# Modulation of shift and scale on VectorE with output channels on partitions, and the start of the first mixer in eighths

## The chip, the core and the metric

One core of a Trainium2 chip runs the whole program. The metric is the device time of one execution in microseconds (us), from a profile of the hardware; three executions are timed, and their median counts.

## The reference

Two decoder layers on 256 tokens of 2048 channels, all float32. A condition vector c modulates each half layer:

```python
cond = silu(c)                                        # 2048
mod = cond @ w_mod[l] + b_mod[l]                      # 2048 x 12288, one product per layer
sh1, sc1, g1, sh2, sc2, g2 = split(mod, 6)
u = x * (1 + sc1) + sh1
proj = u @ w_in[l]                                    # 2048 x 6144: q, k, v, conv gates
# rotary, 8 heads of dilated attention; 8 groups of a gated 3-tap convolution; group RMS norm
x = layer_norm(alpha * x + (1 + g1) * (mixed @ w_out[l]))
u = x * (1 + sc2) + sh2
x = layer_norm(alpha * x + (1 + g2) * (relu(u @ w_ff1[l]) ** 2 @ w_ff2[l]))
```

The matrix w_mod alone is 201 MB, a third of all that is read. Its product is with one vector: each weight is used once.

## The kernel before

**Units, groups and positions.** Every large product is cut into units of 512 output columns. A unit has 8 groups; a group takes one slice of the weights (128 x 1024, 512 KB: two blocks of 128 rows) for both token tiles. TensorE multiplies in three terms, high x high, low x high and high x low, so a group is 12 products of 512 columns (`group`, L1312, products at L1323 to L1325). ScalarE rounds a slice to w_hi (L480), VectorE subtracts to get w_lo (L793); both work four groups ahead (`ahead`). Groups of a layer's mixer are numbered p = 8 * unit + group, and everything beside the groups (rotary, heads, mod steps, slab sums) is put at such a position by hand-written lists: `QK_END`, `Q_AT`, `K_AT`, `HEAD_AT`, `O_AT` (L94 to L102), `MOD_AT` from `mod_positions` (L71), `RED_AT` from `red_positions` (L123). Each engine goes through the positions in this order.

**Modulation.** w_mod is cut into 24 slabs of 1024 output columns, 12 a layer, in 16 chunks of 128 input rows (128 x 1024, 512 KB). Input rows are on partitions. `mod_step` (L799) is one VectorE instruction a chunk: chunk times the column of cond, added to mod_acc (L808; the first of a slab is L804). A slab's 16 steps depend on each other. Then a sum over partitions is still to be made by TensorE. For shift and scale slabs that is `reduce_slab` (L1397): 8 products of 128 x 128 by a column of ones, L1403, two instructions each in the trace; VectorE adds the bias (`reduced`, L832). For the 8 gate slabs (4, 5, 10, 11, 16, 17, 22, 23) it is `gate_slab` (L1407), two products that leave the sum on all partitions, read by `gate_sum` (L839). mod_acc has two halves by turns. The later 20 slabs run through four buffers (mod_raw) that POOL's queue fills, one chunk behind each step that frees one.

**The start.** The first product needs the whole of sh1 and sc1 of layer 0, 4 slabs, so the first mixer begins with `start_units` (L1469): units 0 to 2 run side by side in three pairs of banks, and u comes in quarters. Slab q of the start holds shift and scale of 512 channels; with it 4 blocks of u can be made, and 6 groups (2 of each unit) can run. 64 chunks pass through eight buffers. VectorE does 58 of them as steps; TensorE does 6 directly from the chunk (`start_chunk`, L1431, L1439). `start_fill` (L1462) transposes x, makes the slab's sum (`start_sum`, L1443, L1448) and transposes the second half; `start_scale` (L1010) on VectorE, `start_job` (L506) on ScalarE and `start_low` (L857, L851) turn it into u_hi and u_lo. TensorE waits for u_lo of its block. Within a quarter VectorE's next steps are laid around that by `START_STEPS` and `start_quarter` (L1021).

**Queues.** SyncE's queue carries x, small tables and all layer weights; its first weight slice waits for the fourth mod step (`sp.wait_ge(mod_used, 4)`, L386), later slices for w_lo to free one of four raw buffers. POOL's queue carries w_mod. ScalarE's carries norm gains and gate biases. ScalarE's first work is four weight slices, and only then the first shift and scale of u.

## Time and profile before

| | us |
|---|---|
| median of 3 runs (2360.51, 2363.70, 2363.77) | 2363.7 |
| the profiled execution | 2359.7 |
| its span, first to last instruction | 2358.0 |
| TensorE busy | 2275.1 |
| VectorE busy | 1727.1 |
| ScalarE busy | 1101.9 |
| first product of a group starts at | 42.59 |
| mean granted TensorE clock, share of full | 0.990 |
| moved by DMA | 623 MB, mean 264 GB/s |

The span is what the profiler sees of the instructions; 1.7 us of the execution lie around it. The busy time of an engine is a sum over stages with different limits, so it is read by stage. In timelines a row's second number is how long the instruction (or the run of equal ones, xN) lasted; the start of the next one may come before it has ended, since the engines overlap neighbours. "Idle before" is the time the engine did nothing ahead of it, and the arrow names what ended it.

### The profile page before, as it was taken

Reading aid. Unit: us, or ns where it says so; the run is one execution under the profiler, and the core shown is the slowest. Engines: PE = TensorE matmul, PEld = TensorE weight load, DVE = VectorE, ACT = ScalarE, POOL = GpSimd, SP = SyncE. Lnnn points to the kernel's source line nnn. Section 1 sums busy time; section 2 is a strip of 40 time slices with the busy share of each in tenths; the row PEclk is TensorE's granted clock in tenths of the full one; section 3 lists DMA queues with packets and bytes.
Section 4 is the critical chain, followed back from the end, with each engine's and each line's share of the span. In section 5 each row is a group of like instructions: output and inputs, shape, how many; then the busy total and the mean of one; then the engine's idle time right before and its main releaser. Section 6 shows DMA issues by size and latency. Waiting matters only on the chain.

```text
span 2358.0 us, 30332 instructions
## 1 busy us (share of the span) xinstructions
PE 2275.1 (96%) x10480; PEld 1884.4 (80%) x10480; DVE 1727.1 (73%) x1929; ACT 1101.9 (47%) x1392; POOL 227.3 (10%) x400
## 2 busy tenths in 40 slices
PE   3899999999999999999999999999999999999997
PEld 2777887878888888888878888877888888888886
DVE  6889888877777777668878878777666555555566
ACT  1345543366445445435454554435553543543542
POOL 3311111110001001001010001101000000000000
PEclk9899999999999999999999999999999999999999
DMA  9987888967888888888966888886677776666574
GB/s 379 409 318 274 311 320 313 341 216 255 286 297 287 285 285 300 288 276 289 323 228 196 271 265 288 285 273 224 194 238 239 226 231 212 215 205 195 170 232 133
DMA packets 174734, 623.15 MB, mean 264 GB/s; under 512 B 19728, under 2 KB 20496, under 8 KB 174096
## 3 DMA queue, kind: packets, MB, share of 16 engines
q1 hardware_dynamic: 114128, 407.50, 50.6%
q0 software_dynamic: 55296, 201.35, 25.6%
q10 hardware_dynamic: 5184, 12.59, 1.7%
q8 instruction: 83, 1.36, 0.2%
q14 instruction: 43, 0.35, 0.0%
HBM read 619.27 MB, written 2.10 MB: 264 GB/s over the span
## 4 chain that ended last, share of the span: by engine, by line
PE 87%; DVE 6%; DMA 3%; issue 2%; ACT 1%; ACTq 0%; POOL 0%; DVEq 0%; SPq 0%; POOLq 0%
PE bank L1323 27%; PE bank L1325 26%; PE bank L1324 26%; DMA Z<-w_mod_dram 2%; DVE mod_acc L808 2%; PE bank L1428 2%; DVE w_lo L793 1%; PE bank L1337 1%; PE bank L1403 1%; PE bank L1339 1%; PE bank L1338 1%; ACT w_hi L480 1%; PE bank L1412 1%; DMA raw<-w_out_dram 0%; PE bank L1572 0%
## 5 line engine op out<-in xcount | busy, mean ns | idle before, releaser
L480 ACT ACTIVATE w_hi<-raw 128x1024 fp32r<-128x1024 f32 x764 | 807.6, 1059 | 1135.7 <-PE bank L1325 1015.2
L793 DVE TENSOR_TENSOR w_lo<-raw,w_hi 128x1024 fp32r<-128x1024 f32 x764 | 932.9, 1224 | 550.7 <-ACT w_hi L480 548.9
L1323 PE MATMUL bank<-w_hi,u_hi 128*128 128x512 f32 x1744 | 698.0, 400 | 0.3 <-DVE u_lo L851 0.3
L1325 PE MATMUL bank<-w_lo,u_hi 128*128 128x512 f32 x1744 | 684.1, 392 | 0.0
L1324 PE MATMUL bank<-w_hi,u_lo 128*128 128x512 f32 x1744 | 684.0, 392 | 0.0
L1323 PE MATMUL bank<-w_hi,m_hi 128*128 128x512 f32 x1200 | 470.9, 392 | 4.5 <-DVE m_lo L851 2.6
L1324 PE MATMUL bank<-w_hi,m_lo 128*128 128x512 f32 x1200 | 468.4, 390 | 0.0
L1325 PE MATMUL bank<-w_lo,m_hi 128*128 128x512 f32 x1200 | 468.3, 390 | 0.0
L1325 PEld LDWEIGHTS bank<-w_lo,u_hi 128*128 128x128 f32 x1744 | 330.5, 189 | 70.7
L1323 PEld LDWEIGHTS bank<-w_hi,u_hi 128*128 128x128 f32 x1744 | 330.9, 190 | 68.8 <-issue 1.4
L1324 PEld LDWEIGHTS bank<-w_hi,u_lo 128*128 128x128 f32 x1744 | 331.0, 190 | 68.0 <-issue 1.4
L808 DVE SCALAR_TENSOR_TENSOR mod_acc<-mod_raw,cond,mod_acc 128x1024 f32<-128x1024 f32 x300 | 383.6, 1279 | 0.0
L460 POOL DMA_DIRECT2D mod_raw<-w_mod_dram x316 | 167.0, 528 | 1735.7 <-DVE mod_acc L808 1455.9
L1323 PEld LDWEIGHTS bank<-w_hi,m_hi 128*128 128x128 f32 x1200 | 226.0, 188 | 53.3 <-DVE m_lo L851 3.4
L1325 PEld LDWEIGHTS bank<-w_lo,m_hi 128*128 128x128 f32 x1200 | 226.1, 188 | 47.3
L1324 PEld LDWEIGHTS bank<-w_hi,m_lo 128*128 128x128 f32 x1200 | 226.1, 188 | 46.6 <-issue 0.2
L808 DVE SCALAR_TENSOR_TENSOR mod_acc<-Z,cond,mod_acc 128x1024 f32<-128x1024 f32 x54 | 69.2, 1282 | 13.4 <-DMA Z<-w_mod_dram 11.3
L851 DVE TENSOR_TENSOR m_lo<-utmp,m_hi 128x512 fp32r<-128x512 f32 x72 | 49.1, 691 | 12.8 <-ACT m_hi L504 12.8
L1428 PE MATMUL bank<-idn,Z 128*128 128x128 f32 x416 | 54.1, 273 | 1.2 <-DVE Z L1170 1.1
L1428 PEld LDWEIGHTS bank<-idn,Z 128*128 128x128 f32 x416 | 48.4, 140 | 8.5 <-DVE Z L1170 1.7
L504 ACT ACTIVATE m_hi<-utmp 128x512 fp32r<-128x512 f32 x72 | 45.6, 633 | 2.3
L490 ACT ACTIVATE utmp<-bank 128x512 f32<-128x512 f32 x64 | 37.2, 581 | 0.0
(144 smaller groups left out, 1138.3 us busy)
## 6 DMA issues: line engine op xcount, KB each, us to landing
raw<-w_ff_dram SPq DMA_DIRECT2D x512, 512.0 KB, 4.2
mod_raw<-w_mod_dram POOLq DMA_DIRECT2D x320, 512.0 KB, 5.6
raw<-w_in_dram SPq DMA_DIRECT2D x192, 512.0 KB, 5.3
Z<-w_mod_dram POOLq DMA_DIRECT2D x64, 512.0 KB, 11.0
raw<-w_out_dram SPq DMA_DIRECT2D x64, 512.0 KB, 6.1
gate<-b_rows_dram ACTq DMA_DIRECT2D x4, 1024.0 KB, 5.0
Z<-ln_g_dram ACTq DMA_DIRECT2D x16, 256.0 KB, 6.5
Z<-ln_b_dram ACTq DMA_DIRECT2D x16, 256.0 KB, 7.3
```

The lines of the kernel that those rows point to most:

```text
L460: pool.dma_start(mod_raw[:, k:k + 1, :], chunk(r * MODS + (first + k))).then_inc(mod_in[k], 16)
L480: nc.scalar.activation(weights(w_hi, u_hi, unit, j), raw[:, j % RAW, :], ACT.Copy).then_inc(hi_ready, 1)
L490: nc.scalar.activation(utmp[:, slot, :], tb[bank][:], ACT.Copy).then_inc(t_read[bank], 1)
L504: nc.scalar.activation(dst[:, chunk:chunk + 2, :], utmp[:, slot, :], ACT.Copy).then_inc(split_hi, 1)
L793: nc.vector.tensor_tensor(weights(w_lo, u_lo, unit, j), raw[:, j % RAW, :], weights(w_hi, u_hi, unit, j).bitcast(F32), ALU.subtract).then_ ...
L808: ins = nc.vector.scalar_tensor_tensor(out=a, in0=src, scalar=cond[:, k:k + 1], in1=a, op0=ALU.mult, op1=ALU.add)
L851: nc.vector.tensor_tensor(lo[:, chunk:chunk + 2, :], src, hi[:, chunk:chunk + 2, :].bitcast(F32), ALU.subtract).then_inc(split_ready, 1)
L1323: nc.tensor.matmul(o, hi[:, k, tok], wh, start=(k == 0), stop=False)
L1324: nc.tensor.matmul(o, lo[:, k, tok], wh, start=False, stop=False)
L1325: ins = nc.tensor.matmul(o, hi[:, k, tok], wl, start=False, stop=(k == KC - 1))
L1337: nc.tensor.matmul(o[:], hi[:, k, tok], wh, start=(k == 0), stop=False)
L1428: ins = nc.tensor.transpose(b[:, c * SEQ + t * P:c * SEQ + (t + 1) * P], src(c, t), idn[:])
```

## The change

Shift and scale slabs are turned round on the host: output channels on partitions, input channels along a row. A chunk is now 128 output channels by 1024 of the 2048 inputs, so two chunks make 128 sums. A VectorE step (`column_step`) multiplies the chunk in place by half of cond laid out as a row on all partitions and adds along the row into one column of mod_part; the steps of a slab no longer depend on each other, and two small adds give the biased columns. TensorE has no part in it: `reduce_slab`, `start_chunk` and `start_sum` are gone. To have cond as a row on all partitions, TensorE makes 16 products of a broadcast column of cond by the identity (`spread_condition`) and ScalarE copies them from four banks, once, at the very beginning; the first steps wait for it.

The start goes in eighths: 8 chunks (2 blocks of shift and 2 of scale), then 3 groups, one of each unit. All 64 chunks are VectorE's. Gate slabs are computed as before, with one mod_acc in place of two; the slabs come in another order (`SLAB_ORDER`), so that two gate slabs never follow on each other too closely. The first four later chunks are at position 20 (before 17); the first mixer's mod positions now take 23, 31 and 39 too. Rotary, transposes and heads of the first group of heads move by one to two positions. POOL's start loop is a loop on the engine.

The core of the diff:

```diff
-START_LABELS = GK * START_UNITS
+START_LABELS = START_UNITS
+START_COLS = 2 * GK
+START_LAST = START_LABELS * (EIGHTHS - 1) - 1
...
-    mixer0 = ([17] * 4 + [p for p in range(18, 8 * U_MIX) if p % 8 != 7])[:MIX_SLABS[0] * KC]
+    mixer0 = ([START_LAST] * 4 + [p for p in range(START_LAST + 1, 8 * U_MIX)
+                                  if p % 8 != 7 or p < 40])[:MIX_SLABS[0] * KC]
...
-QK_END = [[(19, 21), (31, 39)], [(7, 15), (31, 39)]]
-Q_AT = [[22, 34], [14, 34]]
-K_AT = [[25, 42], [18, 42]]
-HEAD_AT = [[[27 + 2 * h for h in range(4)], [44 + 2 * h for h in range(4)]],
+QK_END = [[(21, 22), (31, 39)], [(7, 15), (31, 39)]]
+Q_AT = [[24, 36], [14, 34]]
+K_AT = [[27, 42], [18, 42]]
+HEAD_AT = [[[29 + 2 * h for h in range(4)], [44 + 2 * h for h in range(4)]],
...
-O_AT = [[43, 59], [35, 59]]
+O_AT = [[45, 59], [35, 59]]
...
-RED_NOT_BEFORE = {9: MIXER_AT[0] + 8 * U_MIX - 1, 16: MIXER_AT[1] + 8, 17: MIXER_AT[1] + 12}
+RED_NOT_BEFORE = {16: MIXER_AT[1] + 8, 17: MIXER_AT[1] + 12}
+SLAB_ORDER = [4, 6, 5, 7, 8, 9, 10, 12, 11, 13, 14, 15, 18, 16, 17, 19, 20, 21, 22, 23]
...
 def start_order(p):
-    q, i = divmod(p, START_LABELS)
-    return i // GK, GK * q + i % GK
+    e, unit = divmod(p, START_LABELS)
+    return unit, e
...
+            with pool.Fori(1, 2 * START_SLABS) as r:
+                for k in range(8):
+                    pool.wait_ge(mod_used, 8 * r + (k - 7))
+                    pool.dma_start(start_raw[:, k:k + 1, :], chunk(r * 8 + k)).then_inc(start_in[k], 16)
...
+            for i in range(4):
+                act.wait_ge(row_done, i + 1)
+                nc.scalar.activation(cond_row[:, i * NCOL:(i + 1) * NCOL], banks[i][:], ACT.Copy).then_inc(row_ready, 1)
...
+            def column_step(i, src, arrived, landed):
+                dve.wait_ge(arrived, landed)
+                half = slice(i % 2 * SLAB, (i % 2 + 1) * SLAB)
+                nc.vector.scalar_tensor_tensor(out=src, in0=src, scalar=1.0, in1=cond_row[:, half], op0=ALU.mult,
+                                               op1=ALU.mult, accum_out=mod_part[:, i:i + 1]).then_inc(mod_used, 1)
+            def column_sum(col, count, steps):
+                dve.wait_ge(mod_used, steps)
+                part = mod_part[:, 0:2 * count].rearrange("p (c h) -> p c h", h=2)
+                sync(nc.vector.tensor_tensor(mod_col[:, col:col + count], part[:, :, 0], part[:, :, 1], ALU.add))
             def mod_next(q):
+                first = START_SLABS * KC
+                src, arrived, landed = mod_raw[:, q % MODS, :], mod_in[q % MODS], 16 * (q // MODS + 1)
+                n, k = SLAB_ORDER[q // KC], q % KC
+                if n in GATE_SLABS:
+                    gate_step(k, src, arrived, (first + q, landed))
+                else:
+                    column_step(k, src, arrived, landed)
+                    if k == KC - 1:
+                        column_sum(n * SC, SC, first + q + 1)
+                        cols = slice(n * SC, (n + 1) * SC)
+                        nc.vector.tensor_tensor(mod_col[:, cols], mod_col[:, cols], mod_b[:, cols],
+                                                ALU.add).then_inc(columns_done, 1)
...
+            def start_scale(e):
+                col = START_COLS * e
+                column_sum(col, START_COLS, 2 * START_COLS * (e + 1))
...
+                nc.vector.tensor_tensor(u_shift[:, sl], mod_col[:, sh], mod_b[:, sh], ALU.add)
+                nc.vector.scalar_tensor_tensor(out=u_scale[:, sl], in0=mod_col[:, sc], scalar=1.0, in1=mod_b[:, sc],
+                                               op0=ALU.add, op1=ALU.add).then_inc(start_ready, 1)
+            def start_eighth(e):
+                def some(k0):
+                    if e + 1 < EIGHTHS:
+                        start_steps(e + 1, k0, 2)
                     else:
+                        mod_next(k0)
+                        mod_next(k0 + 1)
+                start_scale(e)
+                some(0)
+                start_low(e)
+                some(2)
...
                         for j in range(GROUPS):
                             q, i = divmod(8 * u + j, START_LABELS)
+                            if layer == 0 and q + 1 < EIGHTHS:
+                                if i < 2:
+                                    start_steps(q + 1, 4 + 2 * i, 2)
                                 if i == START_LABELS - 1:
+                                    start_eighth(q + 1)
                             ahead(base + u, j)
                             side(u, j)
...
-            start_mods(0, 0, KC)
-            dve.wait_ge(first_in, 16 * 2)
+            for i in range(2):
+                dve.wait_ge(row_ready, 2 * (i + 1))
+                start_steps(0, i, 1)
+            start_steps(0, 2, 2 * START_COLS - 2)
+            dve.wait_ge(bias_in, 16)
             prepare(0, 0)
+            start_eighth(0)
             prepare(0, 1)
-            start_quarter(0)
             prepare(0, 2)
             prepare(0, 3)
...
-            def reduce_slab(par, job, steps):
-            def start_chunk(q):
-            def start_sum(n):
...
+            def start_fill(e):
+                pe.wait_ge(x_in[e // 2], 16)
+                turn(JOB[("start turn", e)], lambda c, t: xt[:, t, (2 * e + c) * P:(2 * e + c + 1) * P])
+            def spread_condition():
+                pe.wait_ge(cond_ready, 1)
+                for i in range(4):
+                    for c in range(4):
+                        k = 4 * i + c
+                        ins = nc.tensor.matmul(banks[i][:, c * P:(c + 1) * P], cond[:, k:k + 1].to_broadcast([P, P]),
+                                               idn[:], start=True, stop=True)
+                    ins.then_inc(row_done, 1)
...
-    wm = w_mod.reshape(DEPTH, KC, P, 12 * D // 2 // SLAB, SLAB).transpose(0, 3, 1, 2, 4)
+    wm = w_mod.reshape(DEPTH, KC, P, 12 * D // 2 // SLAB, SLAB).transpose(0, 3, 1, 2, 4).reshape(SLABS, KC, P, SLAB)
+    wt = w_mod.reshape(DEPTH, 2, SLAB, 12 * D // 2 // P, P).transpose(0, 3, 1, 4, 2).reshape(SLABS, KC, P, SLAB)
+    wm = np.stack([wm[n] if n in GATE_SLABS else wt[n] for n in list(range(START_SLABS)) + SLAB_ORDER])
```

## Rows read from the trace of the kernel before

**Rows 1.** The page, busy time: engine, us, share of the span, instructions
```profile
PE 2275.1 (96%) x10480; PEld 1884.4 (80%) x10480; DVE 1727.1 (73%) x1929; ACT 1101.9 (47%) x1392; POOL 227.3 (10%) x400
```

**Rows 2.** Stretches: length, busy us and count per engine, granted clock, DMA share, GB/s
```profile
0.00:160.00 160.00, 113.30 (x524) 95.03 (x525) 127.61 (x140) 48.53 (x62) 40.34 (x80) 0.90 0.96 368
160.00:240.00 80.00, 76.15 (x368) 62.40 (x367) 73.32 (x107) 43.23 (x86) 11.60 (x22) 1.00 0.84 301
240.00:2358.00 2118.00, 2085.62 (x9592) 1726.94 (x9590) 1526.21 (x1684) 1010.12 (x1247) 175.32 (x298) 1.00 0.77 255
...
40.00:125.00 85.00, 76.06 (x351) 63.55 (x352) 73.73 (x72) 26.85 (x34) 22.63 (x43) 0.86 1.03 408
140.00:200.00 60.00, 57.25 (x274) 46.68 (x273) 56.31 (x84) 28.70 (x54) 7.92 (x15) 1.00 0.83 297
```

**Rows 3.** TensorE by line: count, busy us and mean ns, idle us before
```profile
L1403 PE MATMUL bank<-ones,mod_acc 128*128 128x1 f32 x192 | 22.1, 245 | 0.7 <-DVE mod_acc L808 0.7
...
L1439 PE MATMUL bank<-cond,Z 128*128 128x1 f32 x96 | 11.6, 250 | 2.0 <-DMA Z<-w_mod_dram 2.0
...
L1583 PE MATMUL bank<-idn,rst 128*128 128x128 f32 x64 | 7.8, 275 | 0.0
```

**Rows 4.** Timeline of TensorE at a column reduction: start us, us, what
```profile
305.52 1.84 PE L1403 MATMUL bank<-ones,mod_acc 128*128 128x1 f32 x16
307.22 0.49 PE L1323 MATMUL bank<-w_hi,u_hi 128*128 128x512 f32 x1
```

**Rows 5.** Timeline of VectorE, start units: cond, fourth step, first and last u_lo
```profile
3.42 0.17 DVE L1286 TENSOR_TENSOR cond<-cc_in,cc_e 128x16 f32<-128x16 f32 x1
...
11.49 1.28 DVE L808 SCALAR_TENSOR_TENSOR mod_acc<-Z,cond,mod_acc 128x1024 f32<-128x1024 f32 x1 [0.25 <-DMA Z<-w_mod_dram]
...
41.85 0.69 DVE L851 TENSOR_TENSOR u_lo<-utmp,u_hi 128x512 fp32r<-128x512 f32 x1 [0.56 <-ACT u_hi L517]
...
132.81 0.69 DVE L851 TENSOR_TENSOR u_lo<-utmp,u_hi 128x512 fp32r<-128x512 f32 x1 [0.34 <-ACT u_hi L517]
```

**Rows 6.** Timeline of ScalarE ahead of the first group
```profile
29.97 1.06 ACT L480 ACTIVATE w_hi<-raw 128x1024 fp32r<-128x1024 f32 x1 [1.50 <-DMA raw<-w_in_dram]
...
40.13 1.02 ACT L513 ACTIVATE utmp<-bank,u_shift,u_scale 128x256 f32<-128x256 f32 x2 [8.91 <-DVE u_scale L1018]
41.18 0.63 ACT L517 ACTIVATE u_hi<-utmp 128x512 fp32r<-128x512 f32 x1
```

**Rows 7.** Timeline of TensorE in the last start groups
```profile
130.72 0.78 PE L1323 MATMUL bank<-w_hi,u_hi 128*128 128x512 f32 x1
...
134.70 0.53 PE L1323 MATMUL bank<-w_hi,u_hi 128*128 128x512 f32 x1
...
151.64 0.39 PE L1324 MATMUL bank<-w_hi,u_lo 128*128 128x512 f32 x1
151.87 0.39 PE L1325 MATMUL bank<-w_lo,u_hi 128*128 128x512 f32 x1
```

**Rows 8.** Timeline of VectorE: small instructions, three dependent steps, steps among w_lo
```profile
39.85 0.17 DVE L1017 COPY u_shift<-mod_col 128x4 f32<-128x4 f32 x1
39.93 0.16 DVE L1018 TENSOR_SCALAR u_scale<-mod_col 128x4 f32<-128x4 f32 x1
...
61.94 4.06 DVE L808 SCALAR_TENSOR_TENSOR mod_acc<-Z,cond,mod_acc 128x1024 f32<-128x1024 f32 x3
...
224.25 1.22 DVE L793 TENSOR_TENSOR w_lo<-raw,w_hi 128x1024 fp32r<-128x1024 f32 x1
225.39 1.28 DVE L808 SCALAR_TENSOR_TENSOR mod_acc<-mod_raw,cond,mod_acc 128x1024 f32<-128x1024 f32 x1
226.59 1.22 DVE L793 TENSOR_TENSOR w_lo<-raw,w_hi 128x1024 fp32r<-128x1024 f32 x1
```

**Rows 9.** Timeline of ScalarE: an accumulator read and the next instruction
```profile
173.69 0.19 ACT L643 ACTIVATION_READ_ACCUMULATOR Z<-Z,nmx 128x1 f32 x1
173.79 0.49 ACT L643 ACTIVATE Z<-Z,nmx 128x256 f32<-128x256 f32 x1
```

More of the change, by code:

```diff
@@ L63 @@
 START_SLABS = 2 * D // SLAB
+START_X = D // NCOL
+EIGHTHS = KC // GK
 MIX_SLABS = (6, 4)
@@ L131, in red_positions @@
         out[p] = n
+    for n, later in zip(GATE_ORDER, GATE_ORDER[1:]):
+        p = next(p for p in out if out[p] == n)
+        assert p < MOD_AT[KC * SLAB_ORDER.index(later)], (n, later)
     return out
@@ L178, in transpose_jobs @@
         modded = layer < DEPTH - 1
-        if layer:
+        if layer == 0:
+            for e in range(EIGHTHS):
+                add(("start turn", e), 1)
+        else:
             add(("fill", 2 * layer), 8)
@@ L188, in transpose_jobs @@
         first, last = MIXER_AT[layer], FF_AT[layer]
-        side += [(p - first, -1, 0, "red", 2 if n in GATE_SLABS else 1, n) for p, n in RED_AT.items()
+        side += [(p - first, -1, 0, "red", 2, n) for p, n in RED_AT.items()
                  if first <= p < last]
@@ L194, in transpose_jobs @@
         side = [(8 * (8 * block + s + 1) + HID_J, "hid", 2, (block, s)) for block in range(BLOCKS) for s in range(4)]
-        side += [(p - last, "red", 2 if n in GATE_SLABS else 1, n) for p, n in RED_AT.items()
+        side += [(p - last, "red", 2, n) for p, n in RED_AT.items()
                  if last <= p < last + 8 * FF_UNITS]
@@ L897, in modulation @@
             def modulation(fill):
-                job = JOB[("red", 12 * (fill // 2) + 6 * (fill % 2) + 3)]
-                dve.wait_ge(t_read[job % 2], job // 2 + 1)
+                first = 12 * (fill // 2) + 6 * (fill % 2)
+                dve.wait_ge(columns_done, 1 + max(COLUMN_ORDER.index(first + i) for i in range(4)))
                 shift = (6 * (fill // 2) + 3 * (fill % 2)) * KC
@@ L1142, in rotate @@
                     dve.wait_ge(pair_used, 8 * base + p + 1)
+                    if layer == 0 and u == 1:
+                        dve.wait_ge(rope_ready, 1)
                     if layer == 0 and u == 0:
@@ L1395, in unit_groups, with gate_slab @@
                         side(j)
-            def reduce_slab(par, job, steps):
-                b = begin_job(job)
-                pe.wait_ge(mod_used, steps)
-                for c in range(SC):
-                    ins = nc.tensor.matmul(b[:, c:c + 1], mod_acc[:, par, c * P:(c + 1) * P], ones[:, 0:1],
-                                           start=True, stop=True)
-                ins.then_inc(t_done, 1)
-            def gate_slab(par, job0, steps):
+            def gate_slab(job0, steps):
                 for i in range(2):
@@ L1429, in turn @@
                 ins.then_inc(t_done, 1)
-            def start_chunk(q):
-                n = q // KC
-                first = q - 1 not in START_PE and all(k // KC < n for k in START_PE if k < q)
-                if first:
-                    pe.wait_ge(sum_read, n)
-                pe.wait_ge(start_in[q % 8], 16 * (q // 8 + 1))
-                for c in range(SC):
-                    ins = nc.tensor.matmul(tb[1][:, c:c + 1], start_raw[:, q % 8, c * P:(c + 1) * P],
-                                           cond[:, q % KC:q % KC + 1], start=(first and c == 0), stop=False)
-                ins.then_inc(chunk_used, 1)
@@ L1469, in start_units @@
             def start_units(side):
+                spread_condition()
                 start_fill(0)
-                for p in range(START_SLABS * START_LABELS):
+                pe.wait_ge(row_ready, 4)
+                for p in range(EIGHTHS * START_LABELS):
                     unit, j = start_order(p)
```

161 lines of the change are left out of this document (42 added, 119 removed).

## The prediction

> **What bounds the kernel now.** I read the page first, then the stretches, then the lines of each engine. The page has TensorE busy 2275.1 us of 2358.0 [rows 1], so 83 us are open. The stretches say where [rows 2]: from 0 to 160 us TensorE is busy 113.3 of 160 (46.7 open), from 160 to 240 it is busy 76.15 of 80, and in the 2118 us behind that 2085.6. Behind 240 us whatever leaves TensorE's queue shortens the run; VectorE has room there (1526 of 2118). Ahead of it two other things are full. From 40 to 125 us the DMA engines move 408 GB/s at a share of 1.03, with VectorE at 73.7 of 85; from 140 to 200 us VectorE is at 56.3 of 60 and TensorE at 57.3. So the kernel is bound by DMA in the start units, by VectorE and TensorE together in the next 80 us, and by TensorE from then on.
>
> **TensorE loses the column reductions.** Twelve later slabs are shift or scale (24 less 4 of the start and 8 gates), and each is reduced by 8 products, 16 instructions in the trace: 192 at L1403 [rows 3]. In the timeline one such block starts at 305.52 and the next group's first product at 307.22 [rows 4]: 1.70 us. 12 x 1.70 = 20.4 us; the busy column gives 22.1 as the upper end. Their positions are 69 and later, so all of them lie behind 240 us, where TensorE is full; nothing covers them. If a layer boundary hides two or three of them the saving is 16, the lower end. VectorE's twelve small reads of them go too and two small adds each take their place, on an engine with room: nothing. I take -20.4.
>
> **The start units.** The chunk products of L1439 [rows 3] and the slab sums of the start go as well, but they stand in a stretch that TensorE does not bound. What counts is when VectorE delivers the last u_lo and what TensorE still has to do then.
> First delivery: VectorE's fourth step starts at 11.49 and ends at 12.8 [rows 5], and only then SyncE issues w_in. The new first step waits for the condition row: cond is ready at 3.6 [rows 5], then 16 spreading products and four copies. The nearest row is L1583, the same kind, 64 instructions (two a product) at 7.8 us [rows 3], so 0.12 us each at full clock and twice that at the low one: 32 of them take 3.9 to 7.4 us, a copy of 512 columns some 0.63, as the rounding at 41.18 [rows 6]. The second half of the row is there between 8.4 and 11.8; I take 10.4. Step two starts there, step four ends at 14.2, and w_in is issued 1.4 later than before. ScalarE took its fourth slice at 29.97 until 31.03 [rows 6], now until 32.4. With 0.3 for the negated sine table, an estimate by its 128 columns, and the shift/scale and the rounding as at 40.13 (1.02 + 0.63) [rows 6], and 0.7 for u_lo, the first delivery is at 35.1. Before it was at 42.5 [rows 5], since all 16 steps of a quarter had to come first. TensorE's first group moves from there to about 35.
> From there to the eighth delivery VectorE has, in its queue's order: 56 steps (64 + 2 less the 10 done), 23 w_lo, 7 u_lo of 0.61 and 7 scale blocks, estimated at 0.45 with their two waits. The trace gives starts, so I use the distance to the next start: w_lo 224.25 to 225.39 is 1.14, a step 225.39 to 226.59 is 1.20 [rows 8].
> The new step's own price is the unknown. The row at 61.94 shows three dependent steps in 4.06, so 1.39 from start to start [rows 8]; the new steps do not depend on each other, which takes that away. What is added is writing the sum. Bounds: at least nothing over 1.14 to 1.20, since it has no scalar column to read; 0.08 for a small VectorE instruction (39.85 to 39.93) [rows 8]; ScalarE shows the same kind of thing as an instruction of its own, 0.19 long and followed 0.10 later by the next [rows 9]. At the top a full 0.20 on 1.20. I take 1.29, near 1.20 + 0.10, since the ScalarE row is the only one that reads an accumulator. Ends 1.20 and 1.40.
> Sum: 56 x 1.29 = 72.2, 23 x 1.14 = 26.2, 7 x 0.61 = 4.3, 7 x 0.45 = 3.2, together 105.9, and 2 for waits on ScalarE: the eighth delivery at 35.1 + 107.9 = 143.0. Before it was at 133.4 [rows 5]. The DMA does not set this: 64 chunks, 27 w_in slices and 2.7 MB besides are 50.4 MB, 124 us at 408 GB/s, so until about 128.
> Behind the eighth delivery only three groups are left where a quarter left six. At full clock a product starts each 0.23 us (151.64 to 151.87); after a pause of some 2.4 us TensorE runs at the lower of its two clocks: from 130.72 to 134.70 there are nine, 0.44 each [rows 7], a surcharge of 2.0. 36 x 0.228 + 2.0 = 10.2, so the last start group ends at 153.2. Before it ended at 151.87 + 0.39 = 152.3 [rows 7], with the first rotated transposes inside. So an earlier beginning by 7 us is given back whole: VectorE takes over six chunks from TensorE, pays the sum on each, and becomes what the start waits for. Net +1, from -7 (1.20 a step, no waits) to +9 (1.40, and 2 more us of waits).
>
> **The next 90 us.** Rotations and heads move by two positions and the mod steps fill positions 23, 31 and 39 too: between positions 24 and 39 there are 16 steps where there were 14, 2.5 us more in a stretch where VectorE is full (from 140 to 200 us) [rows 2]. Slab 5's gate sum leaves it (two adds, 1.3 us). The first slab there is a gate slab, priced as now; column steps begin at position 33, and soon behind that VectorE has slack. I take +1, from -1 to +4.
> Everything else costs nothing: the same bytes in the same packets, the reordered slabs stay ahead of their readers, POOL's loop issues the same DMAs, and 12 x 16 column steps at +0.1 disappear in VectorE's 592 us of slack behind 240. If that cover failed anywhere it would be 0.1 us a step.
>
> **A rule against the change.** In the trace a scalar_tensor_tensor with two f32 sources in SBUF takes 1.28 us beside 1.22 for a tensor_tensor of the same size [rows 8], so two sources do not slow it; no row has it with a sum. The Trainium skill (Vector Engine (DVE) Microarchitecture Reference, section 7) says that this form "with two non-bf16 SBUF sources halves throughput", with no port left for accumulator readback. By that rule the new step, which is just this form with the accumulator, would take twice its time; that is rival 2 below.
>
> **The sum.** The profiled execution: 2359.7 - 20.4 + 1 + 1 = 2341.3. It lies 4.0 under the median of the runs shown (2363.7, from 2360.5), so I say 2345.
>
> **Rivals.**
> 1. *The start gains as well* (chance 0.17): a step costs 1.20 and DMA sets the pace again, so the eighth delivery comes at about 136 and the start ends 7 us earlier; with 22.1 of reductions, 2363.7 - 29 = 2335 or less. For it: independent steps. Against it: VectorE's queue has no gap left in that sum.
> 2. *The accumulating step is slow* (0.06), and the run is slower. Its place is VectorE's queue in the start and in the first mixer. At twice the step, 2.4 us: 56 x 1.1 = 62 us in the start; 64 column steps in the first mixer are 70 more against some 30 of slack there (an estimate: it lacks 6.7 of 80 from 160 to 240 [rows 2] and more behind), so +40; behind that it is hidden. 2363.7 + 62 + 40 - 20 = 2446. It decides from the point where 56 x (step - 1.29) eats the 20 us and 5 more, a step of 1.74 us. For it stands only that no row shows the operation; against it that the same form without the sum costs what its neighbours cost.
> 3. *The gain is eaten* (0.09): a step of about 1.6, or waits of VectorE on ScalarE and on chunks in every eighth (2.5 us each, 18 in all, as VectorE is idle 11 us of the 85 from 40 to 125 now). Then 2363.7 - 20 + 18 = 2361, no difference or nearly none.
> 4. *The change does not take effect in the start*: the first group still comes at 42 because w_in is late. That costs at most 8 us, so 2353, inside the range (0.02).
> The forecast itself, 2337 to 2355, has 0.60; 2355 to 2359 has 0.06.
>
> **The numbers.** What a measurement of this kernel can tell from no change is about 0.2%, 4.7 us. The range 2332 to 2358 leaves out part of rival 1, rival 2 and rival 3. It takes in the bounds: -22.1 - 7 - 1 = -30 below, 2334; -16 + 9 + 4 = -3 above, 2361, whose last 3 us are left out, three ends at once. Faster: forecast, rival 1 and the piece beside it, 0.84; within: 0.09; slower: 0.07.
>
> **What would show it.** The step with its accumulator read in VectorE's lines, about 1.3 from start to start. TensorE's first group at about 35. VectorE nearly without idle time from 40 to 140, and DMA under 400 GB/s there for the first time. The last start group ending within a few us of 153. L1403, L1439, L1448 gone, and TensorE's busy time behind 240 less by some 22. Wrong would be: a step above 1.5; a start that ends over 8 us away from 153; or new TensorE waits for w_lo in the first mixer of more than 5 us.

## The result, and the profile after

The changed kernel took 2336.7 us in the median of four executions (2335.7 to 2341.6), the kernel before 2362.7 (2360.5 to 2363.8): a ratio of 0.9895, 95% interval 0.9883 to 0.9907. It is faster by about 26 us; 2345 was forecast, in a range from 2332 to 2358. The profiled execution took 2336.4, its span is 2334.6.

The page after, busy time; beside it stands [rows 1]:

```profile
PE 2244.9 (96%) x10160; PEld 1851.2 (79%) x10160; DVE 1729.2 (74%) x2215; ACT 1103.2 (47%) x1396; POOL 227.3 (10%) x400
```

TensorE has 30.2 us less of work: 320 instructions fewer (192 of the later reductions, 96 chunk products, 64 slab sums; 32 to spread the condition are new). VectorE's busy time is the same. The same stretches as in [rows 2], the third shorter with the span, and the same columns:

```profile
0.00:160.00 160.00, 106.33 (x424) 85.00 (x425) 135.86 (x226) 53.01 (x69) 40.35 (x80) 0.84 0.98 376
160.00:240.00 80.00, 76.94 (x374) 62.84 (x373) 74.46 (x126) 45.13 (x96) 12.15 (x23) 1.00 0.87 311
240.00:2334.00 2094.00, 2061.60 (x9365) 1703.38 (x9364) 1518.91 (x1865) 1005.03 (x1233) 174.80 (x297) 0.99 0.77 257
40.00:125.00 85.00, 62.63 (x238) 48.96 (x238) 82.15 (x141) 27.35 (x36) 25.30 (x48) 0.86 1.03 409
140.00:200.00 60.00, 55.60 (x265) 44.81 (x264) 57.28 (x89) 27.68 (x54) 8.45 (x16) 1.00 0.86 308
```

In the start (40 to 125 us) VectorE has gone from 73.7 to 82.15 of 85, as forecast, but DMA has not fallen: share 1.03 and 409 GB/s, as before. Both are full. VectorE's lines, with the mean ns of one behind the busy time:

```profile
L817 DVE SCALAR_TENSOR_TENSOR mod_raw<-mod_raw,cond_row 128x1024 f32<-128x1024 f32 x192 | 233.8, 1218 | 0.0
L809 DVE SCALAR_TENSOR_TENSOR mod_acc<-mod_raw,cond,mod_acc 128x1024 f32<-128x1024 f32 x120 | 153.3, 1278 | 0.5 <-DMA mod_raw<-w_mod_dram 0.3
L817 DVE SCALAR_TENSOR_TENSOR Z<-Z,cond_row 128x1024 f32<-128x1024 f32 x64 | 76.2, 1220 | 7.8 <-ACT cond_row L770 5.6 <-DMA Z<-w_mod_dram 2.0
L817 DVE DVE_READ_ACCUMULATOR mod_raw<-mod_raw,cond_row 128x1 f32 x192 | 15.7, 82 | 0.0
```

The step that adds along the row takes 1.22 us, less than the old step's 1.28, which a gate slab still has (L809). The read of the accumulator is an instruction of its own, 0.08 us long. Whether it costs anything is for the timeline of VectorE to say, first in the first eighth and then around the second delivery:

```profile
8.27 1.23 DVE L817 SCALAR_TENSOR_TENSOR Z<-Z,cond_row 128x1024 f32<-128x1024 f32 x1 [4.63 <-ACT cond_row L770]
...
12.81 1.22 DVE L817 SCALAR_TENSOR_TENSOR Z<-Z,cond_row 128x1024 f32<-128x1024 f32 x1
13.96 0.08 DVE L817 DVE_READ_ACCUMULATOR Z<-Z,cond_row 128x1 f32 x1
13.96 1.22 DVE L817 SCALAR_TENSOR_TENSOR Z<-Z,cond_row 128x1024 f32<-128x1024 f32 x1
...
32.55 0.69 DVE L865 TENSOR_TENSOR u_lo<-utmp,u_hi 128x512 fp32r<-128x512 f32 x1 [5.53 <-ACT u_hi L510]
...
48.34 0.69 DVE L865 TENSOR_TENSOR u_lo<-utmp,u_hi 128x512 fp32r<-128x512 f32 x1
...
132.99 0.68 DVE L865 TENSOR_TENSOR u_lo<-utmp,u_hi 128x512 fp32r<-128x512 f32 x1
```

From 12.81 to 13.96 is 1.15 from start to start (over many steps 1.145), and the accumulator read starts together with the next instruction. The sum costs next to nothing, and the step is 0.05 cheaper than the old one. A block of u is delivered when its u_lo ends: the first at 33.2 (forecast 35.1), the eighth at 133.7 (forecast 143.0). Below, a delivery is named by the start of its row, 32.55 and 132.99 here, with 100.4 between them. TensorE at the end of the start:

```profile
133.73 0.50 PE L1335 MATMUL bank<-w_hi,u_hi 128*128 128x512 f32 x1 [2.96 <-DVE u_lo L865]
...
143.40 0.39 PE L1337 MATMUL bank<-w_lo,u_hi 128*128 128x512 f32 x1
145.49 0.50 PE L1335 MATMUL bank<-w_hi,u_hi 128*128 128x512 f32 x1 [1.70 <-DVE Z L1171]
```

The last start group ends at 143.8, 8.5 us sooner than before (152.3 by [rows 7]; forecast 153.2). What the start has gained and what the reductions have, shows where the same product stands in both traces. Each row below lists a product's first and last start, in the kernel before and then in the changed one:

```profile
L1323 PE MATMUL bank<-w_hi,u_hi x1744: 387/389/792, 42.6 to 2255.4; 128*128 128x512 f32 x194
L1323 PE MATMUL bank<-w_hi,m_hi x1200: 389/389/792, 385.4 to 2321.5; 128*128 128x512 f32 x172
```

```profile
L1335 PE MATMUL bank<-w_hi,u_hi x1744: 387/389/796, 33.3 to 2230.4; 128*128 128x512 f32 x194
L1335 PE MATMUL bank<-w_hi,m_hi x1200: 387/389/792, 377.2 to 2296.6; 128*128 128x512 f32 x172
```

The first group that reads m, the input of w_out (377.2), is 8.2 us ahead of before; the last group on this line (2296.6) is 24.9 us ahead. The run's final unit stands on another line and comes behind it; it gives 1.5 us back (its last high x high product starts at 2345.78 before and at 2322.37 after), so 23.4 are left at the end. About a third of the gain is there when w_out begins.

### The profile page after: what moved, and what is told of

It is laid out like the page before. It is cut to its first block, busy times and chain, and to the rows that moved or that the text cites. A ratio compares the mean times of both kernels' runs of the same rounds, so it can differ in the third digit from the quotient of the medians.

```text
span 2334.6 us, 29837 instructions
## 1 busy us (share of the span) xinstructions
PE 2244.9 (96%) x10160; PEld 1851.2 (79%) x10160; DVE 1729.2 (74%) x2215; ACT 1103.2 (47%) x1396; POOL 227.3 (10%) x400
## 4 chain that ended last, share of the span: by engine, by line
PE 84%; DVE 9%; DMA 3%; issue 1%; ACT 1%; ACTq 1%; SPq 0%; DVEq 0%; POOL 0%; POOLq 0%
PE bank L1335 26%; PE bank L1337 25%; PE bank L1336 25%; DVE w_lo L795 3%; PE bank L1428 2%; DVE Z L817 2%; DVE mod_raw L817 1%; PE bank L1349 1%; PE bank L1351 1%; PE bank L1350 1%; DMA Z<-w_mod_dram 1%; DMA raw<-w_out_dram 1%; DMA raw<-w_in_dram 1%; ACT w_hi L486 1%; ACTq L544 1%
## 5 line engine op out<-in xcount | busy, mean ns | idle before, releaser
L817 DVE SCALAR_TENSOR_TENSOR mod_raw<-mod_raw,cond_row 128x1024 f32<-128x1024 f32 x192 | 233.8, 1218 | 0.0
L809 DVE SCALAR_TENSOR_TENSOR mod_acc<-mod_raw,cond,mod_acc 128x1024 f32<-128x1024 f32 x120 | 153.3, 1278 | 0.5 <-DMA mod_raw<-w_mod_dram 0.3
L817 DVE SCALAR_TENSOR_TENSOR Z<-Z,cond_row 128x1024 f32<-128x1024 f32 x64 | 76.2, 1220 | 7.8 <-ACT cond_row L770 5.6
```

Source lines behind the costliest of these rows:

```text
L809: ins = nc.vector.scalar_tensor_tensor(out=mod_acc[:], in0=src, scalar=cond[:, k:k + 1], in1=mod_acc[:], op0=ALU.mult, op1=ALU.add)
L817: nc.vector.scalar_tensor_tensor(out=src, in0=src, scalar=1.0, in1=cond_row[:, half], op0=ALU.mult, op1=ALU.mult, accum_out=mod_part[:, i: ...
```

## The experiments

Two limits were open behind the start: theory D, DMA brings the chunks and slices no faster, and theory V, VectorE's queue. Edits are against the changed kernel unless said otherwise. Times of deliveries come from one profiled execution of each kernel. 

**The first delivery earlier.** ScalarE scales and rounds u ahead of its four slices, VectorE starts the first eighth ahead of the first w_lo:

```diff
+            start_fill(0)
             for j in range(AHEAD):
                 prepare(0, j, first=True)
-            start_fill(0)
...
-            prepare(0, 0)
             start_eighth(0)
+            prepare(0, 0)
```

> The changed kernel with the first eighth's shift and scale, its u_hi and its u_lo made ahead of the first weight slices (ScalarE: start_fill before the four slices; VectorE: start_eighth(0) before the first w_lo). In the changed kernel VectorE stood still for 4.4 us before its first w_lo and 5.5 us before its first u_lo. Theory V (VectorE's queue sets the pace of the start): most of these 10 us are filled, the first group starts at 24 to 26 us in place of 33.3, the eighth u_lo is delivered at about 125 in place of 133, and the whole run is 4 to 8 us shorter than the changed kernel (2336.7), so about 2330. Theory D (the DMA engines, at 409 GB/s there, set it): the first group starts as early, but the last chunk of the start lands when it did, the eighth u_lo comes at 131 to 134 and the run stays at 2335 to 2337.

Measured: 2337.1 us (2336.4 to 2337.3), ratio 0.9888 (0.9871 to 0.9904) to before. The first delivery came at 22.50, ten us sooner, the eighth at 132.87. VectorE did less in the window, DMA the same:

```profile
40.00:125.00 85.00, 59.62 (x222) 46.81 (x223) 79.31 (x136) 28.00 (x36) 24.33 (x46) 0.84 1.03 409
```

VectorE was given 10 us and none of them was left at the eighth delivery: here DMA is the limit. The last chunk of the start landed at 127.2 us in the changed kernel and at 127.3 in this one (landing times of the transfers in the two traces).

**Two small instructions more with every start step.**

```diff
                     column_step(k, start_raw[:, q % 8, :], start_in[q % 8], 16 * (q // 8 + 1))
+                    nc.vector.memset(junk[:, 0, q:q + 1], 0.0)
+                    nc.vector.memset(junk[:, 1, q:q + 1], 0.0)
```

> The changed kernel with two VectorE writes of one column each behind each of the 64 start steps, about 0.14 us together, so that a step costs some 1.29 us, the price that the prediction had taken. Theory V: 56 of them lie between the first and the eighth delivery, so that distance grows by 7 to 8 us (from 100.4 to about 108), the start ends near 151, and the whole run is 5 to 8 us longer than the changed kernel, about 2343. Theory D: the DMA engines had the slack taken from them, the distance grows by 0 to 3 us and the run by 0 to 3.

Measured: 2338.6 us (2337.3 to 2340.2). It did not do what it was made for. The timeline has the two inside the step:

```profile
48.05 1.22 DVE L817 SCALAR_TENSOR_TENSOR Z<-Z,cond_row 128x1024 f32<-128x1024 f32 x1
48.06 0.06 DVE L1022 MEMSET junk<- 128x1 f32 x1
48.07 0.06 DVE L1023 MEMSET junk<- 128x1 f32 x1
49.19 0.08 DVE L817 DVE_READ_ACCUMULATOR Z<-Z,cond_row 128x1 f32 x1
```

A step went from 1.145 to 1.16 and the distance from the first to the eighth delivery from 100.4 to 101.2, so the run tells nothing of VectorE's limit. It had to be made in another way (the dependent steps, below).

**Half of the bytes.** Of chunks 9 to 64 only 512 of 1024 columns are loaded; the step reads old data in the rest, so the sums are others.

```diff
-                    pool.dma_start(start_raw[:, k:k + 1, :], chunk(r * 8 + k)).then_inc(start_in[k], 16)
+                    pool.dma_start(start_raw[:, k:k + 1, 0:NCOL], chunk(r * 8 + k)[:, :, 0:NCOL]).then_inc(start_in[k], 16)
```

> The changed kernel with only half the columns of chunks 9 to 64 of the start loaded (14.7 MB less of 50); the other half of each buffer keeps what an earlier chunk left, so the modulation of the first half layer is not that of the reference. VectorE's work is the same. Theory V: the distance from the first to the eighth u_lo stays at 98 to 100 us (only the waits on chunks, some 2 us, go); DMA falls well under 400 GB/s in the start; the first delivery comes earlier by up to 6 us because the weight slices land earlier. Theory D: the distance shrinks by 10 us or more.

Measured: 2334.5 us in one execution, the eighth delivery at 130.45 instead of 132.99. The distance from the first to the eighth was 99.0 us, in theory V's range of 98 to 100, where theory D had asked for 90 or less. DMA fell to 294 GB/s in the window and VectorE stood at 82.69 of 85. With DMA out of the way VectorE sets the pace, a mere 2.5 us lower. So this run speaks for V as the one before it spoke for D.

**The price of a step.** The edit fell otherwise than its expectation says: the scalar became a column of ones (a pointer) in all start steps and in the even steps of the later shift and scale slabs, all with the sum; the odd later steps have the constant 1.0 and no sum, so half of those sums are left out.

```diff
-            def column_step(i, src, arrived, landed):
+            def column_step(i, src, arrived, landed, plain=False):
...
-                nc.vector.scalar_tensor_tensor(out=src, in0=src, scalar=1.0, in1=cond_row[:, half], op0=ALU.mult,
-                                               op1=ALU.mult, accum_out=mod_part[:, i:i + 1]).then_inc(mod_used, 1)
+                scalar = 1.0 if plain else ones[:, 0:1]
+                kw = {} if plain else dict(accum_out=mod_part[:, i:i + 1])
+                nc.vector.scalar_tensor_tensor(out=src, in0=src, scalar=scalar, in1=cond_row[:, half], op0=ALU.mult,
+                                               op1=ALU.mult, **kw).then_inc(mod_used, 1)
```

> The changed kernel with the two parts of the step's price taken apart. Even start steps have the scalar as a column in SBUF (ones) in place of the constant 1.0, with the sum; odd start steps have the constant and no sum, so half of the sums are missing and the modulation of the first half layer is not that of the reference. If the column is what made the old step 1.20 us from start to start against 1.145 for the new one, the even steps stand at about 1.20 and the odd ones at 1.145. If the sum costs something that the overlap hides only in part, the odd steps are shorter than 1.145; if the overlap is complete they are exactly as long. If the old step was longer for its dependence or for its destination, even steps stay at 1.145.

Measured: 2330.8 us in one execution. An even and an odd later step in its timeline:

```profile
300.26 1.28 DVE L819 SCALAR_TENSOR_TENSOR mod_raw<-mod_raw,ones,cond_row 128x1024 f32<-128x1024 f32 x1
...
301.46 1.22 DVE L795 TENSOR_TENSOR w_lo<-raw,w_hi 128x1024 fp32r<-128x1024 f32 x1
302.60 1.22 DVE L819 SCALAR_TENSOR_TENSOR mod_raw<-mod_raw,cond_row 128x1024 f32<-128x1024 f32 x1
303.73 1.28 DVE L862 SCALAR_TENSOR_TENSOR gate<-bank,gate 128x512 f32<-128x512 f32 x2
```

With pointer and sum 1.20 to the next start, with constant and no sum 1.13, against 1.145 for constant and sum. So the pointer costs 0.06 and the sum at most 0.015: the old step was dearer by its scalar column. In the start every step was at 1.205, 3.4 us more on 56, and the eighth delivery came at 134.25, 1.3 later. The last start group ended no later for it (143.5, after 143.8), because TensorE's clock was higher in it: its products there stand 0.23 apart throughout, where the changed kernel has seven in a row at 0.43. That the run is 5.6 us under the changed kernel's profiled one is for the most part TensorE's clock too (last section).

**Every start step waits for the one before.** From the second eighth on; and in a second kernel behind every second step only.

```diff
                     column_step(k, start_raw[:, q % 8, :], start_in[q % 8], 16 * (q // 8 + 1))
+                    if e > 0:    # the second kernel: if e > 0 and k % 2:
+                        dve.wait_ge(mod_used, q + 1)
```

> Of the changed kernel, VectorE waits behind every start step of eighths two to eight until that step has ended (56 waits); nothing is left out. The old dependent steps stood 1.39 apart, the independent ones 1.145, so each of the 56 steps should cost 0.2 to 0.25 more, 11 to 14 us on VectorE. Theory V (VectorE's queue sets the start, with at most 3 us to spare against DMA): the distance from the first delivery of u_lo to the eighth grows from 100.4 to 110 to 114, the last start group ends at 153 to 157, the run takes 2346 to 2350. Rival D (DMA alone sets it, VectorE has room): the distance grows by under 3 us and the run stays under 2341.

> As the kernel with a wait behind every start step, but behind every second one only (28 waits), so that the mean distance of steps is about the 1.25 to 1.29 that the prediction had taken. Theory V: 5 to 7 us more on VectorE, of which 0 to 3 are covered by DMA: the distance from first to eighth delivery 103 to 107, the last start group ends at 147 to 150. If so, the prediction's formula (steps, w_lo and the rest in one queue) was right and its price was what failed. Rival D: the distance stays at 100 to 101, as then the formula was wrong too.

Measured: 2339.9 and 2341.1 us, one execution each. The wait costs 0.12 a step, not 0.2, as the first kernel's timeline has it:

```profile
50.13 1.22 DVE L817 SCALAR_TENSOR_TENSOR Z<-Z,cond_row 128x1024 f32<-128x1024 f32 x1
...
51.40 1.23 DVE L817 SCALAR_TENSOR_TENSOR Z<-Z,cond_row 128x1024 f32<-128x1024 f32 x1
...
137.36 0.68 DVE L865 TENSOR_TENSOR u_lo<-utmp,u_hi 128x512 fp32r<-128x512 f32 x1
```

56 x 0.12 is 6.7 us more on VectorE; the distance from first to eighth delivery grew by 4.2 (104.6 after 100.4), and the last start group ended at 147.9, 4.1 later. With half of the waits it is 3.4 more on VectorE and the distance grew by 1.1. So VectorE's first 2.3 to 2.6 us more are covered by DMA, and what goes beyond shows in full. The distances are under those that theory V had expected, since the edit's price was about half of the one assumed. Neither theory holds alone. (Both are single executions. That the second kernel took longer in all than the first is TensorE's clock again: at position 24 it was 1.2 us behind the changed kernel, the first 4.1.)

**Both limits relieved.** The early order and the half chunks together; the same part of the sums is left out.

> Of the changed kernel, both edits tried singly before: the first scale and shift of u stand ahead of the first weight slices on ScalarE and VectorE, and of chunks 9 to 64 only half of the columns are loaded, so the step reads old data in the rest (the sums are others). If DMA and VectorE bound the start within 3 us of each other, VectorE can use the earlier beginning only now that DMA is out of the way: four more w_lo behind the first delivery at 22.5 and the same queue else, so the eighth delivery at 125 to 128 (130.5 with half chunks alone, 132.9 with the early order alone) and 2330 to 2333. Rival: something else paces the deliveries (the returns between TensorE, ScalarE and VectorE inside an eighth), then it stays at 129 to 131.

Measured: 2325.9 us in one execution. Deliveries at 21.74, 42.20, 55.87 and so on to

```profile
123.91 0.68 DVE L865 TENSOR_TENSOR u_lo<-utmp,u_hi 128x512 fp32r<-128x512 f32 x1
```

Singly the two brought 0.1 and 2.5 us, together 9.1. That is the mark of two limits side by side, and it is more than was expected. Something third, such as the returns between TensorE, ScalarE and VectorE inside an eighth, would have kept the eighth delivery at 129 or later. Now the pace can be computed. In an eighth VectorE has 8 steps, 3 w_lo, a u_lo and the scale block: 8 x 1.145 + 3 x 1.14 + 0.61 + 0.45 = 13.64 us. DMA has 8 chunks and 3 slices, 11 x 512 KB = 5.77 MB, at 408 GB/s 14.1 us; with half chunks 3.67 MB, 9.0 us. The larger of the two should be the mean distance of the second to the eighth delivery:

| kernel | a step | VectorE | DMA | measured |
|---|---|---|---|---|
| changed | 1.145 | 13.6 | 14.1 | 14.11 |
| slices held back (below) | 1.145 | 13.6 | 14.1 | 14.11 |
| early order | 1.145 | 13.6 | 14.1 | 14.60 |
| half chunks, early | 1.145 | 13.6 | 9.0 | 13.62 |
| half chunks | 1.145 | 13.6 | 9.0 | 13.87 |
| pointer scalar | 1.205 | 14.1 | 14.1 | 14.20 |
| every second step waits | 1.205 | 14.1 | 14.1 | 14.21 |
| every step waits | 1.265 | 14.6 | 14.1 | 14.64 |

All but two rows come out within 0.1. The early order is 0.5 above: its second delivery came 3.1 us sooner than the changed kernel's (45.28, after 48.34), and over the six rounds it fell back to the time at which DMA has brought the chunks. The run with half chunks alone has two rounds of 14.6 among four of 13.5; in the round from 47.26 a w_lo waits 1.02 us for ScalarE's w_hi, so that third path is not always free. The prediction's 1.29 a step would have made VectorE's time 14.8.

**The slices behind the start held back.** SyncE waits for the eighth u_lo ahead of label 25, so that some 2 MB leave the full stretch.

```diff
-                first = 1 if layer == 0 else 0
+                first = 0
+                if layer == 0:
+                    first = 4
+                    for u in range(1, 4):
+                        for j in range(GROUPS):
+                            if (u, j) == (3, 1):
+                                sp.wait_ge(split_ready, EIGHTHS)
+                            load(w_in, u * GROUPS + j, u, j)
```

> Of the changed kernel, SyncE holds the weight slices of labels 25 and later until the eighth u_lo is there, so that some 2 MB, 5 us at 409 GB/s, fall out of the full DMA stretch; nothing is left out. Theory (both limits within 3 us): the eighth delivery comes 2 to 3 us earlier, at 130 to 131, the start ends 2 us earlier and the run takes about 2334.5; VectorE then sets the pace. Rival: the chunks of the last eighths are already under way by then, or the late slices make w_hi and w_lo late behind the start, and the run is as before or up to 4 us slower.

Measured: 2338.9 us (2333.7 to 2341.0), ratio 0.9898 (0.9879 to 0.9918). The eighth delivery stayed at 133.15, and behind the start TensorE waited 4.52 us where it had waited 1.70. The rival happened: these bytes did not stand in the way of the last chunks, and late they hurt a little. I have no version that computes the same and beats the changed kernel.

**The reductions by themselves.** Both against the kernel before: one product of eight (seven eighths of those columns hold old data), and each product twice.

```diff
-                for c in range(SC):
+                for c in range(1):                  # or: list(range(SC)) * 2
                     ins = nc.tensor.matmul(b[:, c:c + 1], mod_acc[:, par, c * P:(c + 1) * P], ones[:, 0:1],
```

> The kernel before, with one of the 8 products of each later column reduction; 7 are left out, so seven eighths of those shift and scale columns hold old data. Theory R (each reduction stands wholly on TensorE's path): 14 of 16 instructions go at 12 places, 0.106 us each by the 1.70 us of a block, so 17.8 us less, up to 19.4 by the 1.85 seen between the two kernels; ratio 0.992 to 0.9925 and 2344 to 2346. With nothing moved in the start this is the prediction's first term by itself. Rival H (part of the reductions is covered by waits at layer boundaries or by VectorE's lag): under 14 us less, 2350 or more.

> The kernel before, with every product of the later column reductions made twice (16 instead of 8, the second overwrites the first; nothing is left out). Theory R: 12 x 1.70 = 20.4 us more, up to 22.2, ratio 1.0087 to 1.0094, 2383 to 2386. Rival H: less than 17 us more. If taking away gives less than adding, the first product of a reduction has a fixed price that stays; the two runs together give the price of a product and of a place.

Measured: 2346.2 us (2342.6 to 2348.4), ratio 0.9936 (0.9916 to 0.9957), and 2408.7 (2406.6 to 2410.9), ratio 1.0204 (1.0186 to 1.0221). Less work behaves nearly as the sum says. By the medians it brought 14.6 us where 17.8 had been worked out, a little outside the forecast of 2344 to 2346. Place by place it is all there: in the first MLP each shortened reduction shows 1.6 us (1.5 had been worked out). New waits for w_lo take 1.9 of 12 x 1.6 = 19.2 back (next section), and the last group on L1323 (first and last start) is 16.7 us ahead of before:

```profile
L1323 PE MATMUL bank<-w_hi,m_hi x1200: 389/389/792, 384.5 to 2304.8; 128*128 128x512 f32 x172
```

The final unit gives 1.5 us back, as in the changed kernel, so 15.2 are left in the profiled execution.

More work costs over twice what it should, and the forecast of 2383 to 2386 is missed: 45.3 us at the last group on L1323 (2366.8) where 20.4 were added. The timeline of TensorE at the first doubled block:

```profile
306.04 3.62 PE L1403 MATMUL bank<-ones,mod_acc 128*128 128x1 f32 x32
309.52 0.49 PE L1323 MATMUL bank<-w_hi,u_hi 128*128 128x512 f32 x1
...
311.01 0.63 PE L1323 MATMUL bank<-w_hi,u_hi 128*128 128x512 f32 x1
311.44 0.63 PE L1324 MATMUL bank<-w_hi,u_lo 128*128 128x512 f32 x1
```

The block itself takes 3.48, twice 1.74, as expected. But 1.5 us behind it products start 0.43 apart instead of 0.23, eight of them: TensorE runs at the lower of its two clocks (1.2 GHz). Stretches around two such places; the granted clock is the third number from the end:

```profile
311.00:315.00 4.00, 4.00 (x12) 3.14 (x11) 2.21 (x4) 1.06 (x1) 1.05 (x2) 0.57 0.75 218
430.00:442.00 12.00, 11.30 (x52) 9.74 (x51) 5.88 (x7) 2.40 (x3) 1.58 (x3) 0.72 1.01 347
```

In the first TensorE is busy throughout, at a clock of 0.57. Such a fall costs the length of the stretch times what the clock lacks, 4 us x 0.43 = 1.7 us here and 12 x 0.28 = 3.4 in the second, where it lasts twice as long. By the granted clock there are 15 such stretches behind 160 us, ahead of the run's end: 11 short ones and 4 long ones, 32 us by that count, where before has 2 short ones (3.4). The 29 us between them and the 20.4 make 49, beside 45.3 measured; the count is an upper end, since it takes in time in which TensorE waits or has only small products. That doubling the products brings the falls is shown by this pair of runs; what it is in the longer block that does it is not.

## Why the prediction held, and where its steps failed

The direction, the range and the main term stood. The start's term failed in size and in sign, and a cost that the sum did not have, TensorE's clock, took back half of what the start gained.

**The column reductions: right, -20.4 forecast, -22 measured.** Between the landmarks of the first MLP each reduction removed shows 1.85 us in my comparison of the traces (7.4 for four). 1.70 is the block; the rest is the product behind it, which starts its follower 0.33 later instead of 0.23 (305.70 to 306.01 behind the shortened block of the experiment). 12 x 1.85 = 22.2, the busy column's bound. They lie on TensorE's path, as the run with one product in eight confirms; by a third run, with the products doubled, the same places can cost more than their own time.

**The start: the step's price failed.** The start was to cost 1 us and saved 8.5, which is outside the stated bounds of -7 to +9. By the prediction's own sign (a start that ends over 8 us away from 153) it was wrong: it ended at 143.8. The prediction took 1.29 from ScalarE's accumulator read, and even its lower end, 1.20, was too high: 1.145, since the old step's excess over a subtraction had been its pointer scalar and VectorE's accumulator read runs beside the next instruction. The prediction had that in sight ("it has no scalar column to read") and let it count only as a bound. 56 x 0.145 = 8.1 us of the 9.3 by which the eighth delivery was sooner than forecast. The first delivery, at 33.2 for 35.1, brought the rest and a little more. Its steps were near: the spreading took 6.06 us for 32 instructions (3.9 to 7.4 were the bounds), step two starts at 10.52 (10.4), step four ends at 14.0 (14.2).

```profile
3.79 6.06 PE L1442 MATMUL bank<-idn,cond 128*128 128x128 f32 x32 [3.79 <-DVE cond L1295]
```

But ScalarE took its fourth slice no later than before (29.97, [rows 6]), where the prediction had added 1.4; why the slices, issued later, did not land later was not tried:

```profile
29.70 1.06 ACT L486 ACTIVATE w_hi<-raw 128x1024 fp32r<-128x1024 f32 x1 [1.50 <-DMA raw<-w_in_dram]
```

**"The DMA does not set this": wrong at the real price.** The total itself was right: done by about 128 was said, and the last chunk landed at 127.2. What was missing is what still follows a chunk that lands: the steps, a w_lo, the scale block and u_lo put the delivery 5.8 us behind it, at 133.0. The formula of VectorE's queue was right as well: with 1.145 a step and the first delivery at 33.2 it gives 33.2 + 97.8 + 2 = 133.0, where 133.7 was measured. With the forecast price it would have ruled; at the real one the two are level, and by eighths DMA is ahead by half a us (14.1 against 13.6). That half us is a sum from bandwidth and bytes; what the runs show is that relieving either limit alone brings 0.1 to 2.5 us and both 9.1. The chain of waits of the changed kernel has both in turn (start, us, what):

```profile
49.03 1.15 DVE Z L817 x2
50.31 0.49 issue
50.83 0.52 POOL Z L442
51.97 12.64 DMA Z<-w_mod_dram
64.63 1.25 DVE Z L817 x2
```

From 78.7 on the chain has no DMA: it runs through VectorE, and in two places (from 91.3 and from 119.4) through the 12 products of a group on TensorE and ScalarE's next w_hi, for which a w_lo waits. The eighth delivery is thus where it was before (132.99, for 132.81 in [rows 5]), and the case is rival 1, which had a chance of 0.17, with its own price of a step even too high. And since only three groups stand behind it in place of six, the start ends 8.5 us sooner instead of 1 later. DMA did not fall under 400 GB/s in the start either (409), as it should have by the prediction's list. "An earlier beginning is given back whole" was half right: it is (the experiment with the early order shows it again), but the shorter tail is not.

**The next 90 us: about right.** +1 was forecast. The lead was 7.3 us at position 24 and 8.5 at 64 in my reading of the traces, so nothing was lost; VectorE is at 57.28 of 60 from 140 to 200.

**The new waits for w_lo: 2.2 us, under the bound of 5.** In the last unit of w_out TensorE now catches up with VectorE:

```profile
464.03 0.50 PE L1349 MATMUL bank<-w_hi,m_hi 128*128 128x512 f32 x1 [0.51 <-DVE w_lo L795]
466.31 0.49 PE L1349 MATMUL bank<-w_hi,m_hi 128*128 128x512 f32 x1 [0.62 <-DVE w_lo L795]
468.99 0.50 PE L1349 MATMUL bank<-w_hi,m_hi 128*128 128x512 f32 x1 [1.03 <-DVE w_lo L795]
```

Three waits at the same place, 1.9 us in all, are in the run with one product in eight, where nothing of the start was changed: they come from the removed reductions.

**The rule against the change.** The rows of before had shown that two f32 sources do not slow the form; the one open case was the sum, and it costs at most 0.015 us (L817). The sentence of the Trainium skill (Vector Engine (DVE) Microarchitecture Reference, section 7) that such an instruction runs at half throughput for want of a port for accumulator readback is not borne out here: 1.145 us for 1024 columns with the accumulator, 1.13 without it.

**The sum against the profiled execution:** start -8.5, reductions -22.2, new waits +2.2, and +4.9 from the clock (last section) make -23.6; measured -23.3 (2359.7 to 2336.4). The last term stood in no step of the prediction. Without it the execution would have come out at 2331.5, which is rival 1's "2335 or less" and under the range's lower end of 2332. So part of the hit is luck: the start came out 9.5 us better than its term of +1, and the clock and the new waits, neither of them in the sum, took 7.1 of that back.

## What to carry to other kernels

Compare the limits of a pipelined stretch by its period: bytes of one round over the bandwidth against the queue time of one round. When totals are compared, add to the transfers what still has to be done behind the last of them. Where two limits lie within a few per cent, taking one away gains next to nothing, and both must go at once. For the price of an untried instruction take what the nearest one lacks as well as what it adds; and when work is added between large products, count the clock that follows it, not the added instructions alone.

## What was not expected of the hardware

- **TensorE's clock falls more often in the faster kernel.** Behind 240 us, and ahead of the idle end of the run, before has two stretches at the lower clock, the changed kernel five. First those of before, then those of the changed one (columns as in [rows 2]; the clock is the third number from the end):

```profile
395.00:404.00 9.00, 8.23 (x37) 6.98 (x38) 6.18 (x10) 3.88 (x5) 1.06 (x2) 0.81 0.90 331
428.00:434.00 6.00, 6.00 (x21) 4.80 (x20) 3.70 (x5) 1.06 (x1) 1.05 (x2) 0.72 1.03 391
```

```profile
316.00:320.00 4.00, 4.00 (x12) 3.08 (x12) 3.69 (x8) 0.21 (x1) 0.53 (x1) 0.61 0.86 275
479.00:485.00 6.00, 5.36 (x19) 4.35 (x20) 5.86 (x11) 4.18 (x9) 4.51 (x2) 0.72 0.64 217
...
1598.00:1605.00 7.00, 6.38 (x24) 5.07 (x25) 5.98 (x11) 5.16 (x12) 5.22 (x2) 0.76 0.69 253
2300.00:2312.00 12.00, 9.86 (x37) 7.64 (x36) 8.22 (x10) 2.57 (x3) 0.00 (x0) 0.86 0.15 48
```

  Length times what the clock lacks gives 3.4 us lost before and 8.3 after (four rows of the five are shown; the fifth is 1203 to 1209, 6 us at 0.72). The first of the five follows a pause of 0.37 us and a block of 16 instructions of one column (L1549, from 313.82 to 315.62); four follow a pause of 2.1 to 2.7 us at the end of a half layer, such as before has too without a fall. In the pointer-scalar run there is one fall (395 to 404, 1.7 us), so by this count 6.6 us less are lost. The positions of its groups agree: it is 0.8 us ahead of the changed kernel at position 64, 3.9 ahead at the last group on the products' line (2292.62 against 2296.56) and 5.5 ahead at the end. Most of it comes, in steps of 0.7 to 1.6 us, where the changed kernel's clock falls and its own does not. So nearly equal work can differ by 5 us or more, and what decides it at a given pause was not tried and stays open.
- **Small independent VectorE instructions are hidden.** A memset of one column issued behind a step began 0.01 us after it and cost 0.01; an accumulator read cost at most 0.015. A pointer scalar in place of a constant cost 0.06 us in 1.145, a wait on the step just issued 0.12.
